# Weights of the top four experts computed behind the first one-hot, and the bias products of the down projection in four row groups

## The chip, the cores and the metric

One core of one Trainium2 chip. A time is the device time of one execution of the whole program in microseconds (us). All data are float32. One execution was also taken by the hardware profiler; the line numbers here are those of that profile.

## What is computed

One step of a decoder layer for 256 prompt tokens and 8 sample tokens, 264 rows in all: a token mixer (retention and gated delta net, with their input projection, branches and output projection), then a mixture of experts, of which the change touches the routing and the bias of the down projection:

```python
logits = x2 @ w_router + b_router                 # 264 x 32
top_v, top_i = lax.top_k(logits, 4)
gate = softmax(top_v)                             # weights of the 4 experts of a token
...
hb  = xb @ w_gate_up[e] + b_gate_up[e]            # 1024 -> 2048
glu = minimum(hb[:, :1024], 7.0)
lin = clip(hb[:, 1024:], -7.0, 7.0)
act = glu * sigmoid(1.702 * glu) * (lin + 1.0)
y   = act @ w_down[e] + b_down[e]                 # 1024 -> 1024
out[token] += gate[token, e] * y
```

The sum over a token's experts of gate * b_down[e] is Z @ b_down, where Z (264 x 32) holds the weights of the chosen experts and zeros elsewhere.

## The kernel before, in words

The program is written engine by engine, each with its own instruction stream in a hand-made order; semaphores order them. The first third is the token mixer. Out of it come `XT`, the residual with features in the partitions, in eight `out_block`s (L1042), and with each block a piece of the router's scores and of the sum of squares (`score`, L1051 and L1053), for which ACT squares `XT` (L1473). The tokens lie in three tiles c = 0, 1, 2 of 128, 128 and 8 rows.

**Routing.** ACT copies scores and sums out (`lgc`, L1475), PE turns them to tokens (L1085), ACT takes the roots of the mean squares into `rs` (L1479), DVE their reciprocals; ACT writes the normed rows `hrow` (L1488) and copies the residual to `X` (L1495). On DVE: `Lg` (L2073), the maxima, `ex` = logits less maximum (L2080), and the mask `sel` of the top four (L2091). From `sel`, PE counts each token's place in its expert's list (L1096, L1097) and the counts (L1100). ACT makes `ex` into exponentials (L1499). DVE makes Z from them (L2094 to L2097: mask, sum, reciprocal, product), then the places `R0` (L2101), the one-hot matrix `O` of block 0 (L2106) and the shifted tables `R` (15 instructions, L2113).

**Blocks.** Block b is 64 slots of expert b. `gather` (L1114) picks its rows with a one-hot; `turn_x` (L1122) transposes them; `gate_up` (L1136) multiplies by 8 chunks `gus` of 1 MB; DVE and ACT form the activation; `turn_act` (L1145), `down` (L1155) with 4 chunks `dns` of 1 MB; `turn_c` (L1165) and `combine` (L1180) spread the 64 rows, weighted, over the tokens in the banks `homes`, and DVE adds them to `X` (L2188). PE's order in iteration b is gate_up(b), turn_act(b-1), turn_c(b-2), gather(b+1), combine(b-2), turn_x(b+1), down(b-1). In iteration 1 nothing is there to combine, and `biases` (L1195) stands in its place: it multiplies ZT, the transposed Z, by `bd`, which holds b_down. ZT is made ahead of `gather(1)`: three transposes (L1208) into bank 6, and a copy by ACT (L1536).

**Loads.** All weights go through SP's queue in this order: `gus` and `dns` of blocks 0 and 1 as the token mixer frees their place, `bd` (L540) ahead of the last of them, then for each block `gus` (L519), the bias `bgu` (L523) and `dns` (L530). There is one set of eight `gus`: the chunk of block b + 1 is issued when gate_up(b) is through with the chunk in its place (`m_guc`). Of `dns` there are two sets; `down(b)` frees those of block b + 2 (`m_dc`). SP waits in order, so a wait for `m_dc` also holds all `gus` behind it.

ACT's functions need tables, and the program holds an ACT_TABLE_LOAD where the next function is not in the one loaded.

Of the kernel before, what the change touches and what calls it, by code (L numbers as in the profile page):

```python
# [14 lines left out]
ALU = mybir.AluOpType  # L15
ACT = mybir.ActivationFunctionType
# [3 lines left out]
AX = mybir.AxisListType  # L20

P = 128
D = 1024
KT = D // P
# [67 lines left out]
def build_layer(nc, d, o):  # L92

    with ExitStack() as ctx:
        base = [-(-nc.sbuf_base // 32) * 32]

        def at(name, offset, shape, dt=F32):
            return nc.alloc_sbuf_tensor_at(name, shape, dt, offset=offset)
# [114 lines left out]
        def mnew(name, shape, dt=F32):  # L213
            n = 4
            for x in shape[1:]:
                n *= x
            t = at(name, mb[0], shape, dt)
            mb[0] += -(-n // 32) * 32
            assert mb[0] <= p0 + PREG, mb[0]
            return t  # L220
# [27 lines left out]
        X, Xd = at("X", ht0, [P, 2, D]), at("Xd", wn0, [NB, D])  # L248
        bd = mnew("bd", [NE, D])
        bgu, ZT = at("bgu", xr0 + 4096, [1, 2, 2, 512]), at("ZT", ed0, [NE, TOK])  # L250
        sg, ac, acT, yb = [at(n, k0 + 4 * C_LVL + 2048 * i, [P, 512]) for i, n in enumerate(("sg", "ac", "acT", "yb"))]
# [128 lines left out]
        def after(eng, s, per, b, plus=0):  # L380

            if isinstance(b, int) and b * per + plus <= 0:
                return
            eng.wait_ge(s, b * per + plus)
# [24 lines left out]
        def _(sp):  # L410
# [128 lines left out]
            sp.wait_ge(s_mix, 8)  # L539
            sp.dma_start(bd[:, :], d["b_down"][0]).then_inc(s_bdn, 16)  # L540
            sp.wait_ge(s_bt, 20)
# [30 lines left out]
        def _(pe):  # L572
# [611 lines left out]
            def biases():  # L1184

                pe.wait_ge(s_ztev, 1)
                pe.wait_ge(s_bdn, 16)
                for c, r in TILES:
                    if c == 1:
                        pe.wait_ge(m_taev, 1)  # L1190
                        pe.wait_ge(m_gxev, 3)
                    elif c == 2:
                        pe.wait_ge(m_b2, 2)
                    for g in range(2):
                        t = pe.matmul(homes[c][g][0:r, :], ZT[:, P * c:P * c + r], bd[:, 512 * g:512 * g + 512],  # L1195
                                      start=True, stop=True)
                    t.then_inc(m_cb, 1)

            pe.wait_ge(s_xaev, 1)
# [7 lines left out]
            for c, r in TILES:  # L1207
                t = pe.transpose(B[6][0:NE, P * c:P * c + r], Z[0:r, c, :], K[0:r, C_ID:C_ID + r])  # L1208
            t.then_inc(s_zt, 1)
# [41 lines left out]
        def _(act):  # L1251
# [218 lines left out]
            for m in range(KT):  # L1470
                act.wait_ge(s_ob, m + 1)
                after(act, s_lg, 1, m - 1)
                nc.scalar.activation(sqt[:, m % 2, :], XT[:, m, :], ACT.Square).then_inc(s_sqt, 1)  # L1473
            act.wait_ge(s_lg, KT)
# [60 lines left out]
            act.wait_ge(s_zt, 1)  # L1535
            nc.scalar.copy(ZT[:, :], B[6][0:NE, 0:TOK]).then_inc(s_ztev, 1)  # L1536
            rows_out(1)
# [136 lines left out]
        def _(dve):  # L1674
# [417 lines left out]
            dve.wait_ge(s_sel, 1)  # L2092
            dve.wait_ge(s_ex, 1)
            link(v.tensor_tensor(ex[:, :, :], ex[:, :, :], sel[:, :, :], ALU.mult))  # L2094
            link(v.tensor_reduce(red[:, :], ex[:, :, :], AX.X, ALU.add))
            link(v.reciprocal(red[:, :], red[:, :]))
            v.tensor_tensor(Z[:, :, :], ex[:, :, :], bc(red[:, :], NE, 2), ALU.mult).then_inc(s_zg, 1)  # L2097

            dve.wait_ge(s_pos, 1)
# [11 lines left out]
            for c, r in TILES:  # L2111
                for m in range(NM):
                    t = v.tensor_scalar(R[0:r, c, NE * m:NE * m + NE], R0[0:r, c, :], -1000.0 - SLOTS * m, None,  # L2113
                                        ALU.add)
            t.then_inc(s_tab, 1)
            dve.wait_ge(s_tab, 3)

# [131 lines left out]
```

## Time and profile before

| | us |
|---|---|
| median of three runs | 1520.24 (1518.2 to 1521.64) |
| the profiled execution | 1520.41 |
| its span, which all views count from | 1518.5 |
| PE busy | 1426.2 |
| DVE busy | 509.3 |
| ACT busy | 247.0 |
| POOL busy | 141.6 |

PE is TensorE, PEld its weight loads, DVE VectorE, ACT ScalarE, POOL GpSimd, SP the engine whose queue issues the loads. A float32 matmul is two instructions (x2) in the views of the trace, a transpose is one.
### The profile page before, as it was taken

The numbers are of one execution on the slowest core, as the hardware profiler recorded it, in microseconds if no ns is written. First come the engines' busy times: TensorE is split into PE (matmuls) and PEld (weight loads), VectorE is DVE, ScalarE is ACT, GpSimd is POOL, SyncE is SP. The second block draws the span as 40 slices with busy tenths as digits, with TensorE's granted clock in tenths as the row PEclk, the third lists the DMA queues.
The fourth block names the chain that finished last, engine by engine and source line by source line (L and its number), as shares of the span: only waits on it lengthen the run. The fifth ranks groups of instructions, "written<-read, shape, count | busy, mean of one in ns | idle before, by whom it ended". The sixth has DMA issues, their size and how long they took to land.

```text
span 1518.5 us, 17635 instructions
## 1 busy us (share of the span) xinstructions
PE 1426.2 (94%) x7230; PEld 690.4 (45%) x7230; DVE 509.3 (34%) x1127; ACT 247.0 (16%) x456; POOL 141.6 (9%) x120
## 2 busy tenths in 40 slices
PE   7998998999999989999999999999999999999996
PEld 6787996448788623333333233233332332233222
DVE  5677534131402212832322242224222422242225
ACT  3342252002210310110110111011101110111012
POOL 1134011010000011001000100010001000100010
PEclk9999999999999998999999999999999999999998
DMA  6513045933546968999999999999999999999991
GB/s 203 211 58 105 35 141 167 292 140 125 181 153 255 357 246 336 417 418 415 417 417 418 415 417 419 417 415 417 418 417 415 416 418 418 415 417 418 417 412 68
DMA packets 129927, 480.46 MB, mean 316 GB/s; under 512 B 16841, under 2 KB 37593, under 8 KB 96777
## 3 DMA queue, kind: packets, MB, share of 16 engines
q1 hardware_dynamic: 129268, 478.68, 79.8%
q8 instruction: 59, 0.97, 0.3%
q0 software_dynamic: 96, 0.33, 0.1%
q10 hardware_dynamic: 480, 0.29, 0.1%
q14 instruction: 24, 0.20, 0.0%
HBM read 468.20 MB, written 11.26 MB: 316 GB/s over the span
## 4 chain that ended last, share of the span: by engine, by line
PE 44%; DMA 41%; SPq 5%; issue 5%; DVE 3%; ACT 1%; POOL 0%; DVEq 0%; ACTq 0%; POOLq 0%
DMA gus<-in_w_gate_up 39%; PE bank L1136 11%; PE bank L647 5%; PE bank L1155 4%; SPq L519 4%; PE bank L1019 4%; PE bank L889 3%; PE bank L620 3%; PE bank L1042 2%; PE bank L635 2%; PE bank L1114 2%; PE bank L1180 2%; DMA Ssg<-in_state_gdn 1%; DVE Ssg L1942 1%; SPq L457 1%
## 5 line engine op out<-in xcount | busy, mean ns | idle before, releaser
L1136 PE MATMUL bank<-gus,xT 128*64 128x512 f32 x2048 | 462.3, 598 | 39.6 <-DMA gus<-in_w_gate_up 37.2
L1136 PEld LDWEIGHTS bank<-gus,xT 128*64 128x64 f32 x2048 | 140.5, 137 | 355.5 <-issue 242.0
L2165 DVE TENSOR_TENSOR glu<-bank,bgb 128x512 f32<-128x512 f32 x32 | 22.1, 691 | 654.5 <-issue 419.1
L1155 PE MATMUL bank<-dns,acT 128*64 128x512 f32 x1024 | 229.2, 600 | 0.0
L1662 POOL PARTITION_BROADCAST bgb<-bgu x32 | 41.6, 1298 | 1042.1 <-DMA bgu<-in_b_gate_up 841.9
L1155 PEld LDWEIGHTS bank<-dns,acT 128*64 128x64 f32 x1024 | 71.2, 138 | 136.8 <-issue 136.8
L647 PE MATMUL bank<-HT,wslot 128*128 128x264 f32 x512 | 119.3, 388 | 0.0
L647 PEld LDWEIGHTS bank<-HT,wslot 128*128 128x128 f32 x512 | 95.3, 190 | 19.6 <-issue 4.6
L1114 PE MATMUL bank<-hrow,O 128*64 128x512 f32 (+1 forms) x384 | 95.4, 615 | 3.5 <-DVE O L2106 3.5
L1520 ACT COPY acT<-bank 128x512 f32<-128x512 f32 x32 | 18.8, 586 | 480.9 <-PE bank L1145 480.9
L1180 PE MATMUL bank<-yb,CT 64*128 64x512 f32 (+1 forms) x384 | 94.5, 607 | 1.7 <-ACT CT L1525 1.6
L635 PE MATMUL bank<-HT,wslot 128*128 128x264 f32 x384 | 89.5, 394 | 0.8 <-DVE HT L1709 0.8
L2188 DVE TENSOR_TENSOR X<-X,bank 128x512 f32<-128x512 f32 x132 | 81.7, 676 | 17.0 <-PE bank L1180 13.1
L635 PEld LDWEIGHTS bank<-HT,wslot 128*128 128x128 f32 x384 | 74.0, 194 | 15.3 <-issue 2.3
L889 PE MATMUL bank<-wslot,HT 128*128 128x512 f32 x128 | 58.9, 620 | 3.7 <-DMA wslot<-in_w_in 3.1
L1180 PEld LDWEIGHTS bank<-yb,CT 64*128 64x128 f32 (+1 forms) x384 | 25.2, 151 | 65.2 <-issue 63.3
L1530 ACT COPY yb<-bank 128x512 f32<-128x512 f32 x32 | 18.8, 587 | 214.1 <-PE bank L1155 214.1
L1114 PEld LDWEIGHTS bank<-hrow,O 128*64 128x64 f32 (+1 forms) x384 | 22.1, 135 | 49.5 <-issue 48.9
L1720 DVE SCALAR_TENSOR_TENSOR uT<-raw,cw,uT 128x256 f32<-128x256 f32 x72 | 42.8, 594 | 2.6
L2188 DVE TENSOR_TENSOR Xd<-Xd,bank 8x512 f32<-8x512 f32 x66 | 41.8, 669 | 2.2 <-PE bank L1195 2.2
L1666 POOL PARTITION_BROADCAST bgb<-bgu x32 | 41.6, 1300 | 6.4 <-POOL bgb L1662 6.4
L889 PEld LDWEIGHTS bank<-wslot,HT 128*128 128x128 f32 x128 | 25.1, 199 | 35.4 <-issue 30.7
(390 smaller groups left out, 1193.4 us busy)
## 6 DMA issues: line engine op xcount, KB each, us to landing
gus<-in_w_gate_up SPq DMA_DIRECT2D x256, 1024.0 KB, 20.6
dns<-in_w_down SPq DMA_DIRECT2D x128, 1024.0 KB, 22.2
wslot<-in_w_in SPq DMA_DIRECT2D x17, 2048.0 KB, 7.9
out<-Ssg SPq DMA_DIRECT2D x8, 512.0 KB, 6.1
Ssr<-in_state_ret SPq DMA_DIRECT2D x4, 1024.0 KB, 11.0
out<-Ssr SPq DMA_DIRECT2D x4, 1024.0 KB, 8.8
wslot<-in_w_branch_b SPq DMA_DIRECT2D x2, 2048.0 KB, 8.4
wslot<-in_w_branch_a SPq DMA_DIRECT2D x2, 2048.0 KB, 8.3
```

The costliest lines, as they stand in the source:

```text
L519: sp.dma_start(gus[k][:, :], expert(d["w_gate_up"], e)[P * k:P * k + P, :]).then_inc(m_wgu[k], 16)
L620: return lambda out, h: pe.matmul(out, lhsT(h), rhs(h), start=True, stop=True)
L635: ins = pe.matmul(B[t % 2][:, 0:TOK], wslot[u][:, k, P * m:P * m + P], HT[:, k, :], start=(k == 0), stop=(k == KT - 1))
L647: t = pe.matmul(B[n % 2][:, 0:TOK], wslot[u][:, k, P * m:P * m + P], HT[:, k, :], start=(k == 0), stop=(k == KT - 1))
L889: t = pe.matmul(banks[c][:, :], lhsT[:, k, P * c:P * c + P], w[:, k, :], start=(k == 0), stop=(k == KT - 1))
L1019: t = pe.matmul(B[m % 2][:, 0:TOK], wslot[r % 2][:, k, P * (m % 4):P * (m % 4) + P], (zT if m < KT else gT)[:, k, :], start=(k == 0), stop ...
L1114: t = pe.matmul(B[3][64 * g:64 * g + 64, :], O[0:r, c, :], hrow[0:r, c, 512 * g:512 * g + 512], start=(c == 0), stop=(c == 2))
L1136: t = pe.matmul(B[part][64 * g:64 * g + 64, :], block_of(xT, k), gus[k][:, D * part + 512 * g:D * part + 512 * g + 512], start=(k == 0), s ...
L1155: t = pe.matmul(B[2][64 * g:64 * g + 64, :], block_of(acT, k), dns[4 * u + k // 2][:, k % 2, 512 * g:512 * g + 512], start=(k == 0), stop= ...
L1180: t = pe.matmul(homes[c][g][0:r, :], CT[64 * g:64 * g + 64, P * c:P * c + r], yb[64 * g:64 * g + 64, :], start=True, stop=True)
L1720: v.scalar_tensor_tensor(acc, raw[:, t % 2, j:j + 256], cw[:, blk, j:j + 1], acc, ALU.mult, ALU.add).then_inc(s_cvc if j < 3 else s_cv, 1)
L2188: t = v.tensor_tensor(f, f, homes[c][g][0:r, :], ALU.add)
```

## The change

1. DVE no longer forms Z ahead of `R0`, `O` and `R`, but behind them.
2. ACT takes a root of the constant `eps` into a column of `red`, which is overwritten later, between two squares; the table of the root is loaded there.
3. `bd` is now 128 partitions by 512: partition group j of 32 holds the half j mod 2 of the columns of b_down, so both halves lie there twice. Four DMAs fill it.
4. ZT lies in 128 partitions, four copies of 32; Z is multiplied by the identity four times for each tile, once into each partition group of bank 6.
5. The bias products of tiles 0 and 1 read four different partition groups of ZT and `bd`, and all wait for `m_taev` and `m_gxev` first; those of tile 2 use groups 0 and 1.

```diff
--- before.py
+++ after.py
@@ -246,8 +246,8 @@
         WN = at("WN", xr0, [P, D])
         wr, br = at("wr", wn0, [P, KT, NE]), at("br", wn0 + 1024, [P, NE])
         X, Xd = at("X", ht0, [P, 2, D]), at("Xd", wn0, [NB, D])
-        bd = mnew("bd", [NE, D])
-        bgu, ZT = at("bgu", xr0 + 4096, [1, 2, 2, 512]), at("ZT", ed0, [NE, TOK])
+        bd = mnew("bd", [P, 512])
+        bgu, ZT = at("bgu", xr0 + 4096, [1, 2, 2, 512]), at("ZT", ed0, [P, TOK])
         sg, ac, acT, yb = [at(n, k0 + 4 * C_LVL + 2048 * i, [P, 512]) for i, n in enumerate(("sg", "ac", "acT", "yb"))]
         gus = [at(f"gus{k}", wreg + 8192 * k, [P, 2 * D]) for k in range(KT)]
         dns = [at(f"dns{k}", (wreg + 65536 if k < 4 else p0 - 32768) + 8192 * k, [P, 2, D]) for k in range(KT)]
@@ -537,7 +537,8 @@
             load_gate_up(0, 0, range(4, 8))
             load_down(1, 1, 1, None)
             sp.wait_ge(s_mix, 8)
-            sp.dma_start(bd[:, :], d["b_down"][0]).then_inc(s_bdn, 16)
+            for j in range(4):
+                sp.dma_start(bd[NE * j:NE * j + NE, :], d["b_down"][0][:, 512 * (j % 2):512 * (j % 2) + 512]).then_inc(s_bdn, 16)
             sp.wait_ge(s_bt, 20)
             load_gate_up(0, 0, range(2))
             sp.wait_ge(s_bt, 24)
@@ -1184,17 +1185,19 @@
             def biases():
 
                 pe.wait_ge(s_ztev, 1)
-                pe.wait_ge(s_bdn, 16)
-                for c, r in TILES:
-                    if c == 1:
-                        pe.wait_ge(m_taev, 1)
-                        pe.wait_ge(m_gxev, 3)
-                    elif c == 2:
-                        pe.wait_ge(m_b2, 2)
+                pe.wait_ge(s_bdn, 64)
+                pe.wait_ge(m_taev, 1)
+                pe.wait_ge(m_gxev, 3)
+                for c in range(2):
                     for g in range(2):
-                        t = pe.matmul(homes[c][g][0:r, :], ZT[:, P * c:P * c + r], bd[:, 512 * g:512 * g + 512],
-                                      start=True, stop=True)
+                        rows = slice(NE * (2 * c + g), NE * (2 * c + g) + NE)
+                        t = pe.matmul(homes[c][g][:, :], ZT[rows, P * c:P * c + P], bd[rows, :], start=True, stop=True)
                     t.then_inc(m_cb, 1)
+                pe.wait_ge(m_b2, 2)
+                for g in range(2):
+                    rows = slice(NE * g, NE * g + NE)
+                    t = pe.matmul(homes[2][g][0:NB, :], ZT[rows, 2 * P:TOK], bd[rows, :], start=True, stop=True)
+                t.then_inc(m_cb, 1)
 
             pe.wait_ge(s_xaev, 1)
             gather(0)
@@ -1205,7 +1208,9 @@
             pe.wait_ge(s_xaev, 4)
             pe.wait_ge(s_zg, 1)
             for c, r in TILES:
-                t = pe.transpose(B[6][0:NE, P * c:P * c + r], Z[0:r, c, :], K[0:r, C_ID:C_ID + r])
+                for j in range(4):
+                    t = pe.matmul(B[6][NE * j:NE * j + NE, P * c:P * c + r], Z[0:r, c, :], K[0:r, C_ID:C_ID + r],
+                                  start=True, stop=True)
             t.then_inc(s_zt, 1)
             gather(1)
             pe.wait_ge(s_xaev, 6)
@@ -1470,6 +1475,8 @@
             for m in range(KT):
                 act.wait_ge(s_ob, m + 1)
                 after(act, s_lg, 1, m - 1)
+                if m == KT - 1:
+                    nc.scalar.activation(red[:, 0:1], eps[:, :], ACT.Sqrt)
                 nc.scalar.activation(sqt[:, m % 2, :], XT[:, m, :], ACT.Square).then_inc(s_sqt, 1)
             act.wait_ge(s_lg, KT)
             nc.scalar.copy(lgc[:, :], B[2][0:64, 0:TOK]).then_inc(s_lgc, 1)
@@ -1533,7 +1540,7 @@
             x_out(0)
             residual_out(4, 6)
             act.wait_ge(s_zt, 1)
-            nc.scalar.copy(ZT[:, :], B[6][0:NE, 0:TOK]).then_inc(s_ztev, 1)
+            nc.scalar.copy(ZT[:, :], B[6][:, 0:TOK]).then_inc(s_ztev, 1)
             rows_out(1)
             sigmoid(0)
             x_out(1)
@@ -2090,12 +2097,6 @@
             link(v.tensor_tensor(eq[:, :, :], eq[:, :, :], R0[:, :, :], ALU.mult))
             v.tensor_tensor(sel[:, :, :], gt[:, :, :], eq[:, :, :], ALU.add).then_inc(s_sel, 1)
             dve.wait_ge(s_sel, 1)
-            dve.wait_ge(s_ex, 1)
-            link(v.tensor_tensor(ex[:, :, :], ex[:, :, :], sel[:, :, :], ALU.mult))
-            link(v.tensor_reduce(red[:, :], ex[:, :, :], AX.X, ALU.add))
-            link(v.reciprocal(red[:, :], red[:, :]))
-            v.tensor_tensor(Z[:, :, :], ex[:, :, :], bc(red[:, :], NE, 2), ALU.mult).then_inc(s_zg, 1)
-
             dve.wait_ge(s_pos, 1)
             for c, r in TILES:
                 t = v.scalar_tensor_tensor(R0[0:r, c, :], B[2][0:r, NE * c:NE * c + NE], 999.0, sel[0:r, c, :],
@@ -2113,6 +2114,11 @@
                     t = v.tensor_scalar(R[0:r, c, NE * m:NE * m + NE], R0[0:r, c, :], -1000.0 - SLOTS * m, None,
                                         ALU.add)
             t.then_inc(s_tab, 1)
+            dve.wait_ge(s_ex, 1)
+            link(v.tensor_tensor(ex[:, :, :], ex[:, :, :], sel[:, :, :], ALU.mult))
+            link(v.tensor_reduce(red[:, :], ex[:, :, :], AX.X, ALU.add))
+            link(v.reciprocal(red[:, :], red[:, :]))
+            v.tensor_tensor(Z[:, :, :], ex[:, :, :], bc(red[:, :], NE, 2), ALU.mult).then_inc(s_zg, 1)
             dve.wait_ge(s_tab, 3)
 
             def extras():
```

Where instructions moved, in the order of each engine. On DVE behind the mask, before (L2094 to L2097 form Z, L2101 `R0`, which the program lists as `R_156`, L2106 `O`, L2113 `R`):

```order
L2091 TENSOR_TENSOR sel<-gt,eq 128x96 [waits dve_chain]
L2094 TENSOR_TENSOR ex<-ex,sel 128x96 [waits s_ex,s_sel]
L2095 TENSOR_REDUCE red<-ex 128x3 [waits dve_chain]
L2096 RECIPROCAL red<-red 128x3 [waits dve_chain]
L2097 TENSOR_TENSOR Z<-ex,red 128x96 [waits dve_chain]
L2101 SCALAR_TENSOR_TENSOR R_156<-bank,sel 128x32 [waits s_pos]
L2101 SCALAR_TENSOR_TENSOR R_156<-bank,sel 128x32
L2101 SCALAR_TENSOR_TENSOR R_156<-bank,sel 8x32
L2106 TENSOR_SCALAR O<-K,R_156 128x64 [waits s_tab]
L2106 TENSOR_SCALAR O<-K,R_156 128x64
L2106 TENSOR_SCALAR O<-K,R_156 8x64
L2110 COPY cnt<-bank 1x32 [waits s_pos]
L2113 TENSOR_SCALAR R<-R_156 128x32 x10
L2113 TENSOR_SCALAR R<-R_156 8x32 x5
```

And now:

```order
L2098 TENSOR_TENSOR sel<-gt,eq 128x96 [waits dve_chain]
L2102 SCALAR_TENSOR_TENSOR R_156<-bank,sel 128x32 [waits s_pos,s_sel]
L2102 SCALAR_TENSOR_TENSOR R_156<-bank,sel 128x32
L2102 SCALAR_TENSOR_TENSOR R_156<-bank,sel 8x32
L2107 TENSOR_SCALAR O<-K,R_156 128x64 [waits s_tab]
L2107 TENSOR_SCALAR O<-K,R_156 128x64
L2107 TENSOR_SCALAR O<-K,R_156 8x64
L2111 COPY cnt<-bank 1x32 [waits s_pos]
L2114 TENSOR_SCALAR R<-R_156 128x32 x10
L2114 TENSOR_SCALAR R<-R_156 8x32 x5
L2118 TENSOR_TENSOR ex<-ex,sel 128x96 [waits s_ex]
L2119 TENSOR_REDUCE red<-ex 128x3 [waits dve_chain]
L2120 RECIPROCAL red<-red 128x3 [waits dve_chain]
L2121 TENSOR_TENSOR Z<-ex,red 128x96 [waits dve_chain]
```

The four instructions of Z, the first of which waits for the exponentials (`s_ex`), went behind `R`; `R0` now waits for PE's positions and the mask alone.

On ACT from the squares on, before:

```order
L1473 ACTIVATE sqt<-XT 128x264 [waits s_ob] x2
L1473 ACTIVATE sqt<-XT 128x264 [waits s_lg,s_ob] x6
L1475 COPY lgc<-bank 64x264 [waits s_lg]
L1479 ACT_TABLE_LOAD
L1479 ACTIVATE rs<-bank,eps 128x2 [waits s_lt]
L1479 ACTIVATE rs<-bank,eps 8x1
```

And now:

```order
L1480 ACTIVATE sqt<-XT 128x264 [waits s_ob] x2
L1480 ACTIVATE sqt<-XT 128x264 [waits s_lg,s_ob] x5
L1479 ACT_TABLE_LOAD [waits s_lg]
L1479 ACTIVATE red<-eps 128x1 [waits s_ob]
L1480 ACTIVATE sqt<-XT 128x264
L1482 COPY lgc<-bank 64x264 [waits s_lg]
L1486 ACTIVATE rs<-bank,eps 128x2 [waits s_lt]
L1486 ACTIVATE rs<-bank,eps 8x1
```

The table load left the place ahead of the roots of L1479 (now L1486) and stands ahead of a root of one column; it waits for `s_lg`, the root for `s_ob`, and the eighth square follows them.

On PE the bias products, before:

```order
L1195 MATMUL bank<-bd,ZT 128x512 [waits s_bdn,s_ztev]
L1195 MATMUL bank<-bd,ZT 128x512
L1195 MATMUL bank<-bd,ZT 128x512 [waits m_gxev,m_taev]
L1195 MATMUL bank<-bd,ZT 128x512
L1195 MATMUL bank<-bd,ZT 8x512 [waits m_b2]
L1195 MATMUL bank<-bd,ZT 8x512
```

And now:

```order
L1194 MATMUL bank<-bd,ZT 128x512 [waits m_taev,m_gxev,s_bdn,s_ztev]
L1194 MATMUL bank<-bd,ZT 128x512 x3
L1199 MATMUL bank<-bd,ZT 8x512 [waits m_b2]
L1199 MATMUL bank<-bd,ZT 8x512
```

The first row waits for all that tiles 0 and 1 need; after it four products of 128 rows follow one another without a wait.

## Rows read from the trace of the kernel before

**Rows 1.** The page, GB/s moved by DMA in 40 equal slices.

```profile
GB/s 203 211 58 105 35 141 167 292 140 125 181 153 255 357 246 336 417 418 415 417 417 418 415 417 419 417 415 417 418 417 415 416 418 418 415 417 418 417 412 68
```

**Rows 2.** Chain that ended last, at the roots and near the end: start us, us, what.

```profile
522.90 0.77 issue
...
1449.92 26.86 DMA gus<-in_w_gate_up
```

**Rows 3.** Stretches of 4 us: busy of PE, PEld, DVE, ACT, POOL; PEclk, DMA share, GB/s.

```profile
524.00:528.00 4.00, 3.13 (x23) 2.03 (x21) 3.45 (x18) 3.69 (x8) 0.00 (x0) 1.00 0.80 328
...
532.00:536.00 4.00, 2.41 (x6) 0.85 (x8) 2.72 (x25) 0.00 (x0) 0.00 (x0) 0.61 0.00 0
...
544.00:548.00 4.00, 4.00 (x20) 1.29 (x18) 0.00 (x0) 1.26 (x1) 0.00 (x0) 1.00 0.34 123
...
580.00:584.00 4.00, 4.00 (x7) 1.37 (x5) 1.28 (x2) 0.00 (x0) 0.00 (x0) 0.58 1.02 418
584.00:588.00 4.00, 4.00 (x5) 0.36 (x4) 1.28 (x2) 0.00 (x0) 0.00 (x0) 0.50 0.81 338
...
592.00:596.00 4.00, 4.00 (x16) 1.19 (x14) 0.00 (x0) 0.00 (x0) 0.00 (x0) 0.71 0.47 134
```

**Rows 4.** SP's queue in order of time: start us, us, line, operation.

```profile
503.36 17.69 SPq L519 DMA_DIRECT2D gus<-in_w_gate_up  x4
...
545.23 12.34 SPq L519 DMA_DIRECT2D gus<-in_w_gate_up  x8
...
593.02 6.24 SPq L530 DMA_DIRECT2D dns<-in_w_down  x4
```

**Rows 5.** ACT in order of time, same columns, idle before and its releaser in brackets.

```profile
522.37 1.28 ACT L1479 ACT_TABLE_LOAD   x1
523.67 0.40 ACT L1479 ACTIVATE rs<-bank,eps 128x2 f32<-128x2 f32 x2
...
579.23 0.59 ACT L1505 COPY xg<-bank 128x512 f32<-128x512 f32 x1 [1.17 <-PE bank L1114]
```

**Rows 6.** DVE in order of time, around the exponentials.

```profile
527.71 0.26 DVE L2091 TENSOR_TENSOR sel<-gt,eq 128x96 f32<-128x96 f32 x1
531.51 0.26 DVE L2094 TENSOR_TENSOR ex<-ex,sel 128x96 f32<-128x96 f32 x1 [3.54 <-ACT ex L1499]
...
532.47 0.37 DVE L2101 SCALAR_TENSOR_TENSOR R<-bank,sel 128x32 f32<-128x32 f32 x3
...
533.47 1.35 DVE L2113 TENSOR_SCALAR R<-R 128x32 f32<-128x32 f32 x15
```

**Rows 7.** PE in order of time, from the positions to down(0).

```profile
529.02 0.22 PE L1097 MATMUL bank<-sel,K 8*8 8x32 f32 x2
...
533.59 4.25 PE L1114 MATMUL bank<-hrow,O 128*64 128x512 f32 x12 [3.46 <-DVE O L2106]
...
539.96 0.49 PE L1208 MATMUL bank<-K,Z 128*32 128x128 f32 x3
540.38 2.94 PE L1114 MATMUL bank<-hrow,O 128*64 128x512 f32 x12
...
579.11 9.22 PE L1195 MATMUL bank<-bd,ZT 32*128 32x512 f32 x12
...
589.30 9.55 PE L1155 MATMUL bank<-dns,acT 128*64 128x512 f32 x32
```

**Rows 8.** PE: prices of column and row groups, timeline, then the chain.

```profile
22.42 1.10 PE L600 MATMUL bank<-HT,wab 128*32 128x264 f32 x16
...
400.22 1.15 PE L983 MATMUL bank<-dq,kms 32*128 32x256 f32 x16
401.30 3.83 PE L647 MATMUL bank<-HT,wslot 128*128 128x264 f32 x16
...
207.68 1.78 PE bank L620 x16
...
619.88 7.02 PE bank L1155 x32
```

## Prediction

> **What bounds the kernel now.** I read the page's 40 slices first. From slice 16 of 40 (607 us) to the last but one, the DMA engines move 412 to 419 GB/s whatever the other engines do; before that the numbers are uneven [rows 1]. The chain that ended last agrees: in its last half it is a row of loads of `gus`, 25 to 27 us long each, one for a block, with little between them [rows 2]. So the end is the start of a full-rate stream plus its bytes. A faster matmul behind 607 us buys nothing; what buys time is DMA idle time that goes away before that.
>
> The table by stretch shows that idle time [rows 3]. The stream slows in 524 to 528 and stands still until 544 to 548 (123 GB/s in 4 us, at 418 GB/s that is 1.2 us of work, so it resumes at 546.8). It runs full from there, and stops again at 587.2 (338 GB/s in 584 to 588 is 3.2 us of work), to resume at 594.7 (134 GB/s in 592 to 596 is 1.3 us). I call them gap 1 and gap 2; gap 2 is 7.5 us. Between them lie 40.4 us of full-rate traffic, the 16 MB of gate/up weights of blocks 1 and 2.
>
> What ends each gap is in the queue of SP [rows 4]. Gap 1 ends when the first product of block 0, at L1136, frees `gus`: the first reload is issued at 545.23, data flow 1.6 us later. Gap 2 ends when the first quarter of `down(0)`, L1155, frees `dns`: issued at 593.02, flowing 1.7 us later. What the change touches lies in front of these two points.
>
> **The change, part by part.**
>
> *The square root's table.* Before, ACT loads it at 522.37 behind the copy of `lgc`, and the root starts at 523.67 [rows 5]. The scores' transposes were through at 522.90 and the chain counts 0.77 us of mere issue from there [rows 2]: that is what the load costs. In the changed order the load waits for the product of score 5, and falls between two squares while PE still has out block 7 to do (3.8 us), so it is covered. The new root of one column waits for `s_ob` and stands ahead of the last square. The two roots after the load took 0.40 us together, so I give the new one 0.2 us, of which 0.1 us is covered because PE is at the row transposes. Gain: 0.65 us. Without that cover it would be 0.55.
>
> *First one-hot ahead of the weights.* `sel` is written at 527.71, and DVE then stands for 3.54 us until ACT has the exponentials; the four instructions of Z, then L2101, and `gather(0)` on PE follow at 533.59 [rows 6, 7]. What L2101 itself needs is the last L1097, which ended at 529.24. It could start at 529.30 in place of 532.47: 3.17 us. PE's own counts (L1100) had ended 3.46 us before `gather(0)`, at 530.1 [rows 7], or 529.5 with the 0.65, and `gather(0)` would come at 529.8: they don't hold it up. Z now stands behind the 15 instructions of R (1.35 us [rows 6]). With both shifts, R ends near 531.1, the exponentials are there at 530.8, and Z, a microsecond of work, is ready at 532.1. PE asks for it behind `gather(0)` and two sets of transposes, at about 535. Three microseconds of cover hide it; the second one-hot, which is queued behind Z on DVE, waits for `gather(0)` anyway.
>
> *The clock at `gather(0)`.* That group took 4.25 us, the same group for block 1 2.94 us [rows 7]. In front of the first PE was idle for 3.46 us, and the granted clock of 532 to 536 is 0.61 [rows 3], so a good part of the group ran at 1.2 GHz. With 0.3 us of idle time left I expect 2.4 GHz: 1.31 us more. The bounds are 0 and 1.31.
>
> *Z transposed into four partition groups.* Three transposes took 0.42 us [rows 7]. Now they are 12 matmuls, eight of 128 columns. The only matmuls into four column groups in the trace are those of L600: eight of 264 columns, 2112 in all, in 1.10 us [rows 8]. 1024 columns are then 0.5 us, the four 8-column ones at most 0.2. That is 0.7, or 0.3 more than now; I take 0.4. If they ran one by one, L620's rate of eight 128-column matmuls in 1.78 us [rows 8] gives 2.0 us, 1.6 more. The nearest row is L600, with the same groups.
> The Trainium skill (TensorE: Matmul & The Clock Gate, Terms) says of the transpose mode that it is "4× faster for FP32", which speaks against giving it up. Here a transpose of 128 columns took a third of 0.42 us and L620 0.22 us, 1.5 times as much, so the trace does not bear it out; by the rule the eight would be 1.2 us in two sets of four, and the time 0.5 us longer.
>
> So `gate_up(0)` comes earlier by 0.65 + 3.17 + 1.31 - 0.4 = **4.7 us**, and so does the end of gap 1, one for one: the weights of block 0 had all landed by 528 [rows 3] and are needed from 538.5.
>
> *The load of `bd`.* Four issues in place of one, 256 KB in place of 128 KB: 0.3 us at 418 GB/s. They stand ahead of the first gate/up loads, but those are issued over 17.7 us and waited for `s_bt` [rows 4], and the queue had emptied 11 us before the first use. Nothing. Without that cover it costs 0.3 us and three issues.
>
> *The bias products.* From L1195 at 579.11 to L1155 at 589.30 are 10.2 us, and 13.9 us to the first freed `dns` [rows 7, 4]. Six matmuls of 32 rows run one after the other, and the granted clock fades under them: 0.58 in 580 to 584, then 0.50 until down is well under way [rows 3]. Now four matmuls stand in four row groups and write to four banks. The row to price them by is L983, eight matmuls of 32 rows by 256 columns in four row groups into four banks: from 400.22 to L647 at 401.30 [rows 8], 1.08 us for 2048 columns. L647 needs 3.76 us for 2112 one by one. The bias products of c = 0 and 1 are 4 x 512 = 2048 columns: 1.1 us. The two for c = 2 go in a pair, as the six of L1114 do in 2.94: 1.0 us.
> Their wait moves ahead: it now holds c = 0 too until ACT has copied `xg` of block 2, from 579.23 for 0.59 us [rows 5]. That is 0.7 us of idle PE. Only this and the transposes of turn_x(2) are queued behind it.
> At 2.4 GHz the way from the start of the biases to the first freed `dns` is 0.7 + 1.1 + 1.0 + 0.6 (four transposes, half of what they took at 1.2 GHz) + a quarter of 7.02 (down at 2.4 GHz [rows 8]) = 5.2 us, in place of 13.9. It starts at 579.1 - 4.7 = 574.4, so the load is issued at 579.6 and flows at 581.3. The traffic already queued lasts until 587.2 - 4.7 = 582.5. **Gap 2 closes whole**, with 1.2 us to spare, and gives its 7.5 us. PE gains more (some 14 us up to `gate_up(2)`), which it only spends in waiting sooner for weights.
>
> *Sum:* 4.7 + 7.5 = 12.2 us, out of 1520.41 us for the profiled execution (span 1518.5 and 1.9 around it): 1508.2. The median shown is 0.2 lower; forecast **1508.0 us**.
>
> **The rivals.**
> - *The clock still falls at the biases.* For it: it fell within 2 us of their start, and it fell after the 2.3 us pause ahead of `gate_up(1)` too; the new pause of 0.7 us and the half-filled pair remain. Against: they last 2 us in place of 9, two times as dense and more. Then the way is 0.7 + 2 x 4.5 = 9.7 us, data flow at 585.8, and 3.3 us of gap 2 stay: 12.2 - 3.3, **1511.3 us**. Chance 0.18.
> - *The row groups don't overlap, so that the change doesn't do what it says.* L983 speaks against it. Then the old 13.9 us and the 0.7 us of wait: gap 2 grows by 0.7, gain 4.7 - 0.7 = 4.0, **1516.2 us**. Chance 0.06.
> - *Routing gains little, because gather(0) or its clock is held by something that I don't see*; only gap 2 closes: **1512.7 us**. Chance 0.06.
> - *Slower: the clock falls and stays at 1.2 GHz through down(0) and gate_up(2).* Down(0) then takes 14.0 us, gate_up(2) 27.5 us, from 594.4 to 621.9; the next `dns` is freed only 9 us of products later, near 630.9, flowing at 632.5. Before, 12 MB after 594.7 reached 624.8, so the stream is 7.7 us behind: **1527.9 us**. It decides from a low clock of about 27 us on. The rows show recovery within 5 us of dense work, both at `gather(0)` and at down(0) (0.71 in 592 to 596). Chance 0.03.
>
> **How the numbers follow.** The forecast has the rest, 0.67, of which I keep 0.04 for gains that vanish in something not seen. A measurement can tell 0.2%, 3 us, from no change. Faster by more: 0.63 + 0.18 + 0.06 + 0.06 = 0.93, less 0.01 for the serial case coming out smaller: 0.92. Within: 0.05. Slower: 0.03. The range: the lower end is the sum without the charge for Z and with 1.5 us for the scatter of three runs (1518.2 to 1521.64), 1506; the upper takes in the clock's rival and L620's price for Z, 1511.3 + 1.2, and the routing rival: 1513. Outside are the serial case, no change and slower, 0.13 to 0.15.
>
> **What would show it.** ACT: a table load between the squares of L1480, none at L1486. DVE: L2102 some 0.1 us behind the last L1098, no wait of 3.5 us. PE: `gather(0)` near 529.8, some 2.9 us long; `gate_up(0)` near 538.5; L1194 and L1199 together about 2 us from 575.1, clock 1.00; down(0) 7.0 us. DMA: resuming near 542, then no 4 us stretch under 380 GB/s up to the end, whose rate is again 415 to 418 GB/s. It would be wrong if the stream's rate fell, if gap 2 stayed at full length, or if L1194 took over 4 us.

## The result, and the profile after

The changed kernel takes **1510.18 us** (median of four runs, 1508.32 to 1513.36) against 1520.24 us: the ratio is 0.9935, with a 95% interval of 0.9919 to 0.9951. That is 10.1 us faster, where 12.2 us was forecast (1508.0 us), and inside the range of 1506 to 1513. The profiled execution is the slowest of the four, 1513.36 us with a span of 1511.4 us, so it explains 7.1 us. The other 3 us are found further down, in later profiles of the same kernel.

The page's row of GB/s, in slices of 37.8 us now. From slice 16 on it reads as in [rows 1]; the two slices ahead of it rose.

```profile
GB/s 197 220 58 95 46 130 167 288 158 126 168 167 226 392 250 385 418 416 414 418 418 416 416 418 417 416 416 417 417 417 416 417 417 417 415 418 417 417 410 66
```

The stretches of 4 us (busy of PE, PEld, DVE, ACT, POOL; PEclk, DMA share, GB/s), against [rows 3]:

```profile
524.00:528.00 4.00, 3.52 (x31) 2.84 (x28) 3.45 (x18) 3.69 (x8) 0.00 (x0) 1.00 1.01 422
528.00:532.00 4.00, 3.63 (x24) 2.52 (x26) 2.57 (x24) 3.38 (x6) 0.00 (x0) 0.88 0.07 27
532.00:536.00 4.00, 3.22 (x10) 0.47 (x7) 1.16 (x6) 0.58 (x1) 0.00 (x0) 0.69 0.00 0
...
540.00:544.00 4.00, 4.00 (x20) 1.19 (x22) 0.00 (x0) 1.87 (x2) 0.00 (x0) 1.00 0.13 16
544.00:548.00 4.00, 4.00 (x22) 1.40 (x20) 0.00 (x0) 0.00 (x0) 2.32 (x2) 1.00 0.86 350
...
576.00:580.00 4.00, 3.22 (x16) 0.44 (x12) 2.59 (x8) 0.58 (x1) 0.00 (x0) 0.85 1.02 422
580.00:584.00 4.00, 4.00 (x12) 1.49 (x12) 3.20 (x8) 0.58 (x1) 0.00 (x0) 0.50 1.01 414
584.00:588.00 4.00, 4.00 (x18) 1.32 (x16) 0.00 (x0) 0.00 (x0) 1.77 (x2) 0.79 0.52 165
588.00:592.00 4.00, 4.00 (x22) 1.26 (x18) 0.00 (x0) 0.58 (x1) 0.83 (x1) 1.00 1.01 412
592.00:596.00 4.00, 4.00 (x20) 1.26 (x18) 0.00 (x0) 0.00 (x0) 0.00 (x0) 1.00 0.94 336
```

Gap 1 now ends in 544 to 548, where 350 GB/s are 3.35 us of work at 418: the stream resumes at 544.7, 2.1 us earlier than before. Gap 2 has shrunk: 165 GB/s in 584 to 588 leave 2.4 us idle, in place of 7.5. A new small hole follows in 592 to 596, 336 GB/s, 0.8 us: the four `dns` are through before `gate_up(2)`, which starts at 590.4, has freed its first chunk. Two stretches have a low clock where I expected 1.00: 532 to 536, at `gather(0)`, and 580 to 584, at the biases.

DVE around the mask, against [rows 6]:

```profile
527.72 0.26 DVE L2098 TENSOR_TENSOR sel<-gt,eq 128x96 f32<-128x96 f32 x1
529.36 0.37 DVE L2102 SCALAR_TENSOR_TENSOR R<-bank,sel 128x32 f32<-128x32 f32 x3 [1.39 <-PE bank L1098]
529.77 0.57 DVE L2107 TENSOR_SCALAR O<-K,R 128x64 f32<-128x64 f32 x3
...
530.36 1.35 DVE L2114 TENSOR_SCALAR R<-R 128x32 f32<-128x32 f32 x15
531.63 0.24 DVE L2118 TENSOR_TENSOR ex<-ex,sel 128x96 f32<-128x96 f32 x1
...
532.41 0.26 DVE L2121 TENSOR_TENSOR Z<-ex,red 128x96 f32<-128x96 f32 x1
```

L2102 starts 0.1 us behind the positions, Z (L2118 to L2121) is written at 532.7. ACT around the roots, against [rows 5]:

```profile
517.18 0.42 ACT L1480 ACTIVATE sqt<-XT 128x264 f32<-128x264 f32 x1 [3.90 <-DVE XT L2071]
517.63 1.28 ACT L1479 ACT_TABLE_LOAD   x1
521.51 0.20 ACT L1479 ACTIVATE red<-eps 128x1 f32<-128x1 f32 x1 [2.60 <-DVE XT L2071]
521.62 0.41 ACT L1480 ACTIVATE sqt<-XT 128x264 f32<-128x264 f32 x1
522.78 0.37 ACT L1482 COPY lgc<-bank 64x264 f32<-64x264 f32 x1 [0.76 <-PE bank L1054]
523.68 0.40 ACT L1486 ACTIVATE rs<-bank,eps 128x2 f32<-128x2 f32 x2 [0.53 <-PE bank L1086]
```

The table load (L1479) falls between two squares, while PE has out block 7 to do. The new root takes 0.20 us, and the square starts at 521.62.

PE, against [rows 7], and SP's two issues that end the gaps, against [rows 4]:

```profile
530.48 4.59 PE L1115 MATMUL bank<-hrow,O 128*64 128x512 f32 x12 [0.34 <-DVE O L2107]
...
537.28 0.82 PE L1212 MATMUL bank<-K,Z 128*32 128x128 f32 x24
538.03 2.94 PE L1115 MATMUL bank<-hrow,O 128*64 128x512 f32 x12
540.90 13.95 PE L1137 MATMUL bank<-gus,xT 128*64 128x512 f32 x64
...
577.60 1.14 PE L1194 MATMUL bank<-bd,ZT 32*128 32x512 f32 x8 [0.78 <-ACT xg L1512]
578.67 1.77 PE L1199 MATMUL bank<-bd,ZT 32*8 32x512 f32 x4
580.38 1.12 PE L1123 MATMUL bank<-K,xg 128*128 128x128 f32 x4
581.42 9.17 PE L1156 MATMUL bank<-dns,acT 128*64 128x512 f32 x32
```

```profile
542.88 12.35 SPq L519 DMA_DIRECT2D gus<-in_w_gate_up  x8
...
585.15 5.86 SPq L530 DMA_DIRECT2D dns<-in_w_down  x4
```

Both ends of the gaps moved with the issue: 545.23 to 542.88, and 593.02 to 585.15.

Executions differ in the token mixer ahead of all this by up to 4 us, a part that the change does not touch. So I count from the end of the last score product (the last L1053 or L1054), which lies at 521.94 before and 522.74 here. In the table, all times are us from there, worked out from each kernel's PE rows; "end" is the span less that point. "Old" biases are the six products in one row group, "new" the six in four groups.

| kernel (profile) | gather(0) starts, takes | gate_up(0) starts | biases, us | down(0) starts, takes | end |
|---|---|---|---|---|---|
| before | 11.65, 4.25 | 21.31 | old, 9.22 | 67.36, 9.55 | 996.6 |
| changed | 7.74, 4.59 | 18.16 | new, 1.14 and 1.77 | 58.68, 9.17 | 988.7 |
| changed, second | 7.74, 4.93 | 20.89 | new, 1.14 and 1.03 | 58.51, 7.09 | 988.9 |
| changed, third | 7.74, 4.59 | 18.16 | new, 1.14 and 1.03 | 57.47, 7.09 | 986.1 |
| e1, order and table | 7.74, 4.59 | 17.74 | old, 8.60 | 63.17, 8.47 | 992.1 |
| e2, bias part | 11.64, 4.42 | 21.88 | new, 1.14 and 1.03 | 61.10, 7.09 | 991.3 |
| e3, table | 10.86, 4.93 | 21.20 | old, 8.44 | 66.46, 8.63 | 995.3 |
| e4, late biases | 7.74, 4.59 | 18.16 | none here | 55.36, 7.09 | 986.1 |
| e5, filler | 8.12, 2.94 | 18.17 | new, 1.14 and 1.03 | 57.48, 7.09 | 985.9 |
| e6, spare PE work | 7.75, 4.99 | 20.90 | new, 1.14 and 1.03 | 58.52, 7.09 | 990.3 |
| e7, late and filler | 8.13, 2.94 | 18.18 | none here | 55.38, 7.09 | 986.3 |
| e8, filler, Z early | 8.12, 2.94 | 16.99 | new, 1.14 and 1.03 | 54.61, 7.09 | 985.2 |
| e9, e8 and late | 8.12, 2.94 | 16.99 | none here | 52.49, 7.09 | 985.0 |

### The profile page after: what moved, and what is told of

Same layout as the page of the kernel before. It is cut to its first block, busy times and chain, and to the rows that moved or that the text cites. A ratio compares the mean times of both kernels' runs of the same rounds, so it can differ in the third digit from the quotient of the medians.

```text
span 1511.4 us, 17681 instructions
## 1 busy us (share of the span) xinstructions
PE 1419.1 (94%) x7251; PEld 688.0 (46%) x7251; DVE 508.8 (34%) x1127; ACT 247.0 (16%) x457; POOL 141.5 (9%) x120
## 4 chain that ended last, share of the span: by engine, by line
PE 44%; DMA 42%; SPq 5%; issue 5%; DVE 3%; ACT 1%; POOL 0%; DVEq 0%; ACTq 0%; POOLq 0%
DMA gus<-in_w_gate_up 39%; PE bank L1137 11%; PE bank L648 5%; PE bank L1156 4%; SPq L519 4%; PE bank L1020 4%; PE bank L890 3%; PE bank L621 3%; PE bank L1043 2%; PE bank L636 2%; PE bank L1115 2%; PE bank L1181 2%; DMA Ssg<-in_state_gdn 1%; DVE Ssg L1949 1%; DMA wslot<-in_w_in 1%
## 6 DMA issues: line engine op xcount, KB each, us to landing
Ssr<-in_state_ret SPq DMA_DIRECT2D x4, 1024.0 KB, 11.4
```

## The experiments

**Each part alone.** e1 has the order and the table, with the biases of before:

```diff
+                if m == KT - 1:
+                    nc.scalar.activation(red[:, 0:1], eps[:, :], ACT.Sqrt)
...
-            dve.wait_ge(s_ex, 1)
-            link(v.tensor_tensor(ex[:, :, :], ex[:, :, :], sel[:, :, :], ALU.mult))
...
             dve.wait_ge(s_pos, 1)
...
             t.then_inc(s_tab, 1)
+            dve.wait_ge(s_ex, 1)
+            link(v.tensor_tensor(ex[:, :, :], ex[:, :, :], sel[:, :, :], ALU.mult))
...
```

> The routing part alone: Z behind the one-hot, and the root's table between the squares; the bias products and their loads are those of before. Theory (the time is DMA idle time ahead of a full-rate stream): gather(0) starts 3.9 us earlier relative to the last score product, and gate_up(0) and the end of gap 1 follow, by 3.5 to 5 us, less if the clock falls again at gather(0); gap 2 keeps its 7.5 us, because the biases and down(0) shift along with it. Ratio 0.997 to 0.998, 1515.5 to 1517. Rival (the whole gain of 10 us comes from the biases, and routing is hidden by something): ratio 1.000.

Measured: 1514.86 us against 1520.44, ratio 0.9966 (0.9954 to 0.9978), 5.6 us, just under the 1515.5 to 1517 expected; by their profiles the ends in the table are 4.5 us apart. PE in its profile:

```profile
527.93 4.59 PE L1114 MATMUL bank<-hrow,O 128*64 128x512 f32 x12 [0.34 <-DVE O L2102]
...
573.78 8.60 PE L1195 MATMUL bank<-bd,ZT 32*128 32x512 f32 x12
...
583.36 8.47 PE L1155 MATMUL bank<-dns,acT 128*64 128x512 f32 x32
```

`gather(0)` starts 7.74 us behind the last score product, in place of 11.65: the 3.9 us of the theory. It takes 4.59 us, so the clock fell again (0.54 in 528 to 530). The old biases take 8.6 us, and 6.7 us of gap 2 are left. The rival (routing is hidden) falls.

e2 is the changed kernel with these two edits (the order on DVE and the table) undone.

> The bias part alone: four row groups, Z transposed four times, four loads of b_down; the routing order and the root's table are those of before. Theory: gate_up(0) comes 0.4 us later (the 24 small matmuls of Z), the biases take 2 to 3 us in place of 9.2 behind a wait of 0.7 us, and gap 2 shrinks from 7.5 to between 0 and 3.5 us: ratio 0.9955 to 0.9975, 1513.5 to 1516.5. With e1 it sums to the whole change. Rival (the two parts need one another): the sum of the two gains falls short of 10 us by more than 2 us.

Measured: 1514.85 us, ratio 0.9960 (0.9946 to 0.9974), 5.6 us. In its profile the biases take 1.14 and 1.03 us, and down(0) runs in 7.09 us. gate_up(0) starts 21.88 us behind the last score, 0.57 later than before: Z's 24 small instructions, and a `gather(0)` that happened to be 0.2 us longer. The sum of the two gains, 11.2 us, is that of the whole change (10.1) within the intervals, so the parts don't need one another.

e3 has the table alone.

> Only the square root's table is loaded between the squares; everything else is the kernel before. Theory: the roots at L1479 start 0.7 to 0.8 us sooner behind the last score, but DVE's one-hot is still behind the exponentials, which are behind the copies on ACT's queue, so the shift is passed on whole: 0.7 us, ratio 0.9995, not to be told from none. Rival (the loads of tables cost more than their row shows, as an engine may have to drain at each): 2 us or more, ratio 0.9985 or less.

Measured: 1518.92 us, ratio 0.9991 (0.9982 to 1.0000). The profile gives the price: `gather(0)` starts 10.86 in place of 11.65 us behind the last score, 0.79 us. Its clock took 0.68 us of that back in this execution, and most of the 1.3 us by which its end is sooner comes from a shorter gap 2. The median moved by 1.5 us. The rival's 2 us or more are inside the interval, so the time alone does not exclude them, but the rows speak against them: before, the first root started at 523.67, right behind the load that ran from 522.37 for 1.28 us [rows 5].

**Where the biases stand.** e4 takes them out of iteration 1, and puts them and DVE's additions behind down(15), with semaphores of their own:

```diff
                 else:
-                    biases()
+                    pe.sem_inc(m_cb, 3)
...
                 down(b - 1, (b - 1) % 2, 16 * ((b - 1) // 2) + 16)
+                if b == LATE:
+                    biases(b)
```

> The whole change, with the bias products and their additions moved from iteration 1 to iteration 16, behind down(15), where PE waits for weights anyway. Nothing is left out. Theory: gap 2 closes, since down(0) starts some 3 us sooner and its first dns is freed ahead of the time when the queue is empty; in iteration 16 PE and DVE have 2 us of products and 4 us of additions more, which the lead of the loads covers. 2 to 4 us faster than the changed kernel: ratio 0.991 to 0.992, 1506.5 to 1508. Rival (what is left of gap 2 in the changed kernel costs nothing, since the stream makes it up): the same as the changed kernel, 0.9935. Rival (the pause in iteration 16 starves the stream): slower than the changed kernel.

Measured: 1510.98 us, ratio 0.9939 (0.9925 to 0.9952): no faster than the changed kernel. The profile does what the theory says. In iteration 1 and then in iteration 16:

```profile
576.04 0.66 PE L1125 MATMUL bank<-K,xg 128*128 128x128 f32 x4 [0.69 <-ACT xg L1515]
576.63 7.09 PE L1158 MATMUL bank<-dns,acT 128*64 128x512 f32 x32
```

```profile
1025.76 1.03 PE L1194 MATMUL bank<-bd,ZT 32*8 32x512 f32 x4
1026.72 1.14 PE L1199 MATMUL bank<-bd,ZT 32*128 32x512 f32 x8
1030.55 9.64 PE L1139 MATMUL bank<-gus,xT 128*64 128x512 f32 x36 [2.70 <-DVE X L2220]
```

down(0) starts 3.3 us sooner than in the changed kernel's first profile, and no 2 us stretch between 544 and 640 is under 380 GB/s. In iteration 16 PE stands for 2.7 us behind DVE's additions, and the stream does not notice: no stretch of 4 us from 640 to 1460 falls below 380 GB/s. The 2 to 4 us that I expected did not come. The likely reason is that gap 2 was closed in most executions of the changed kernel already, and that only those like its first profile had something left to win. That asked for more profiles of the changed kernel.

> The changed kernel once more, on the chip of e5 to e7, since its first profile was the slowest of its four runs. Theory (the clock at the biases falls in some executions and not in others, as it did in the first profile and did not in e2's): a median of 1509.5 to 1511, and, if the profile catches an execution without the fall, gap 2 closed and a span 3 us shorter than the first profile's. Rival (the first profile is typical): 1512 to 1514.

Measured: 1510.37 us (1506.23 to 1512.01), ratio 0.9932 (0.9918 to 0.9946). Gap 2 is closed in its profile, but the low clock at `gather(0)` lasted longer (0.50 in 530 to 538, 0.53 in 538 to 540), so gate_up(0) came 2.7 us later than in the first profile, and the ends, 988.7 and 988.9, are nearly the same. The changed kernel a third time, beside e8 and e9:

> The changed kernel on the chip of e8 and e9, as their measure: 1509.5 to 1511, ratio 0.993 to 0.994.

Measured: 1510.57 us, ratio 0.9943 (0.9930 to 0.9957). PE in the third profile:

```profile
530.30 4.59 PE L1115 MATMUL bank<-hrow,O 128*64 128x512 f32 x12 [0.34 <-DVE O L2107]
...
537.10 0.82 PE L1212 MATMUL bank<-K,Z 128*32 128x128 f32 x24
...
577.41 1.14 PE L1194 MATMUL bank<-bd,ZT 32*128 32x512 f32 x8 [0.78 <-ACT xg L1512]
578.49 1.03 PE L1199 MATMUL bank<-bd,ZT 32*8 32x512 f32 x4
...
580.03 7.09 PE L1156 MATMUL bank<-dns,acT 128*64 128x512 f32 x32
```

Here the biases are through in 2.1 us and down(0) takes 7.09 us, at 2.4 GHz. In both later profiles no 2 us stretch between 552 and 640 is under 380 GB/s: gap 2 is closed whole, as forecast. The third one's end is 986.1, as e4's. Over all profiles with the new biases in iteration 1 the clock fell at them in one of seven, the first; with the old ones in three of three.

**What the end hangs on.** e6 gives PE idle products in the second half of the stream:

```diff
+                if b >= 16:
+                    spare(3)
```

`spare(3)` is three products of 128 rows by 256 columns into bank 7.

> The changed kernel with three idle products of 128 rows by 256 columns more in each of the iterations 16 to 31, 1.3 us each time, 20 us of PE work in all. Their results are not used. Theory (behind about 770 us the stream of weights sets the end, and PE's 2.4 us of waiting in each block covers the extra work): the changed kernel's time, up to 2 us more for what lies in the last block. Rival (PE is the bound and the stream follows it): 20 us slower.

Measured: 1511.35 us, ratio 0.9942 (0.9928 to 0.9957), 1.0 us above the changed kernel in the same comparison. The stretch from 1200 to 1450, in e6 and then in the changed kernel's second profile:

```profile
1200.00:1450.00 250.00, 244.21 (x1129) 85.00 (x1127) 71.44 (x154) 27.98 (x50) 20.75 (x16) 1.00 1.02 417
```

```profile
1200.00:1450.00 250.00, 236.81 (x1082) 75.54 (x1080) 71.63 (x156) 27.74 (x51) 20.75 (x16) 1.00 1.02 417
```

PE is busy 7.4 us more, and the stream is at 417 GB/s in both. A group of three takes 1.30 us up to the next instruction, 21 us for the 16 groups; the busy time of PE over the whole span rose by only 11.8 us (1418.0 to 1429.8), and why it rose by so much less stays open. By either count the added work cost about one microsecond, so PE is not the bound there: the rival falls. Most of the microsecond lies behind the stream, where one of the groups stands: from the last eight instructions of gate_up(31) to the end of the span are 42.5 us in e6, and 41.4 and 41.7 in the changed kernel's second and third profile.

**The clock at gather(0).** In e5 the counts go behind `gather(0)`, and wide products fill their place:

```diff
+            pe.wait_ge(s_hrev, 6)
+            pe.matmul(B[7][:, 0:256], ident, XT[:, 0, 0:256], start=True, stop=True)
             pe.wait_ge(s_sel, 1)
...
-            for c, r in TILES:
-                t = pe.matmul(B[1][:, 0:NE], K[0:r, C_ONE:C_ONE + P], sel[0:r, c, :],
...
+            pe.matmul(B[7][:, 0:512].rearrange("p (a n) -> p a n", a=2), ident, XT[:, 2:4, 0:256], start=True, stop=True)
...
             gather(0)
+            for c, r in TILES:
+                t = pe.matmul(B[1][:, 0:NE], K[0:r, C_ONE:C_ONE + P], sel[0:r, c, :],
...
```

> The changed kernel with PE kept at wide work around the positions: the counts of L1101, which gather(0) does not need, go behind it; in their place stands one product of 128 rows by 512 columns of the residual with the identity, and one of 256 columns ahead of the positions, both into bank 7, which is overwritten later. Nothing is left out. In the traces so far gather(0) took 4.3 to 4.9 us at 1.2 GHz even where PE had stood still for only 0.3 us. Theory (the clock falls because the work of the last microseconds is narrow or small, and not because of the pause alone): with the filler the clock stays at 2.4 GHz, gather(0) takes 2.9 us, gate_up(0) comes 1.5 us sooner, and the median is 1 to 2 us below the changed kernel's. Rival (only the pause or the place in time counts): gather(0) takes 4.6 us again and the time is the changed kernel's, within 0.5 us.

Measured: 1510.31 us, ratio 0.9937 (0.9924 to 0.9949), the changed kernel's time and not the 1 to 2 us less that I expected.

```profile
527.69 0.70 PE L1094 MATMUL bank<-XT,K 128*128 128x256 f32 x2 [0.45 <-ACT hrow L1499]
...
529.27 1.13 PE L1102 MATMUL bank<-XT,K 128*128 128x512 f32 x2
530.58 2.94 PE L1114 MATMUL bank<-hrow,O 128*64 128x512 f32 x12 [0.18 <-DVE O L2111]
...
537.01 0.82 PE L1216 MATMUL bank<-K,Z 128*32 128x128 f32 x24 [1.14 <-DVE Z L2125]
```

The clock stayed: `gather(0)` takes 2.94 us, at 2.4 GHz. The filler changes two things, though. It puts wide products among the narrow ones, and it shortens PE's two pauses, from 0.51 and 0.34 us to 0.45 and 0.18, so e5 alone does not show which of the two holds the clock. e2 bears on it, where the products of 32 columns (L1097 to L1101) run from 529.33 to 531.67 and the pause of 3.22 us follows them:

```profile
529.20:531.00 1.80, 1.67 (x16) 1.51 (x16) 0.08 (x1) 1.80 (x5) 0.00 (x0) 1.00 0.05 23
531.00:531.60 0.60, 0.60 (x4) 0.49 (x3) 0.00 (x0) 0.58 (x2) 0.00 (x0) 0.57 0.00 0
```

The clock is down (0.57) while the narrow products still run, ahead of the long pause, with only 0.51 us of idle time right in front of them. And the pause of 0.78 us ahead of the new biases, which stands behind the wide products of a gather, left the clock at 1.00 when they started, in all seven profiles. So the narrow work counts, and the long pause is not needed. No run has the narrow work without any pause.

But the gain went into a new wait: the counts come later, DVE copies them ahead of R and Z, and PE stands 1.14 us for Z at L1216. gate_up(0) starts at 18.17 us, where it did in the first and third profile.

e7 joins e4 and e5.

> The late bias products of e4 and the filler of e5 together. Nothing is left out. Theory: gap 2 stays closed whatever the clock does, and gap 1 ends 1.5 us sooner than in e4 if the filler holds the clock: 1 to 2 us under e4, ratio 0.9925. Rival: the same as e4, 0.994.

Measured: 1510.08 us, ratio 0.9932 (0.9920 to 0.9944). The rival holds (e4's ratio was 0.9939): e7 has e5's wait for Z, and its end is 986.3.

e8 mends that wait:

```diff
             t.then_inc(m_O, 1)
+            dve.wait_ge(s_ex, 1)
+            link(v.tensor_tensor(ex[:, :, :], ex[:, :, :], sel[:, :, :], ALU.mult))
...
             dve.wait_ge(s_pos, 2)
             v.tensor_copy(cnt[:, :], B[1][0:1, 0:NE]).then_inc(s_tab, 1)
...
-            dve.wait_ge(s_ex, 1)
-            link(v.tensor_tensor(ex[:, :, :], ex[:, :, :], sel[:, :, :], ALU.mult))
...
```

> e5 with DVE's four instructions of Z put back ahead of the copy of the counts and of R, but still behind the one-hot of block 0. Nothing is left out. In e5 the filler held the clock, but the counts came later, R and Z with them, and PE stood 1.14 us ahead of the transposes of Z, so gate_up(0) came 18.2 us after the last score product, as in the changed kernel where its clock fell for a short while (18.2 us; 20.9 us where it fell for long). Theory: Z no longer waits for the counts, the pause goes, and gate_up(0) comes 17.0 us after the last score product; the median is 1 us under e5 and 1 to 3 us under the changed kernel, 1507.5 to 1509.5, ratio 0.992 to 0.993. Rival (the first third of the program scatters more than that, and the gain cannot be told): within 0.5 us of the changed kernel.

Measured: 1509.17 us (1506.62 to 1510.10), ratio 0.9929 (0.9915 to 0.9942).

```profile
530.97 2.94 PE L1114 MATMUL bank<-hrow,O 128*64 128x512 f32 x12 [0.18 <-DVE O L2111]
...
536.20 0.82 PE L1216 MATMUL bank<-K,Z 128*32 128x128 f32 x24
536.97 2.94 PE L1114 MATMUL bank<-hrow,O 128*64 128x512 f32 x12
539.84 13.95 PE L1136 MATMUL bank<-gus,xT 128*64 128x512 f32 x64
```

The wait is gone, gate_up(0) starts 16.99 us behind the last score product, as expected. It is 1.4 us under the changed kernel beside it (1510.57), with intervals that overlap. e9 adds the late biases:

> e8 with the late bias products of e4. Nothing is left out. Theory: as e8, and gap 2 is closed in every execution and not only in those where the clock holds at the biases: 0 to 1.5 us under e8, ratio 0.992. Rival: the same as e8.

Measured: 1508.99 us (1506.77 to 1510.14), ratio 0.9934 (0.9920 to 0.9948): e8's time. Both medians are below all three of the changed kernel (1510.18, 1510.37, 1510.57). By the traces they start the stream 1.2 us sooner than its best profile, but these runs alone don't settle that they are faster.

## Why the prediction was nearly right

- *The bound* was right: DMA idle time ahead of a full-rate stream. The sum can be made from the table for each profile: what gate_up(0) gained plus what gap 2 lost. For the third profile of the changed kernel that is 3.15 + 7.5 = 10.65 us, and the end moved by 10.4; for the first 3.15 + 7.5 - 2.4 - 0.8 = 7.45, and it moved by 7.9; for e8 4.32 + 7.5 = 11.8 and 11.4. In e1 and e3 the slow stretch at the old biases was a little shorter, and 0.8 and 1.1 us of gap 2 went: 3.57 + 0.8 = 4.4 against 4.5, and 0.11 + 1.1 = 1.2 against 1.3. For the second profile it is 0.42 + 7.5 = 7.9, and 7.7. Only e2 misses, -0.57 + 7.5 = 6.9 against 5.2. Most of its 1.7 us were lost behind the full-rate stream: in stretches of 2 us the rate first falls under 380 GB/s 40 us ahead of the end of the span before, and 42 us ahead of it in e2. Why, stays open.
- *The table*: 0.65 us forecast, 0.79 measured in e3. The 0.1 us that I charged for the late square was not there.
- *The order*: 3.17 us forecast; together with the table `gather(0)` was to come 3.82 us sooner and came 3.91 sooner.
- *The clock at gather(0)* is the term that failed. "With 0.3 us of idle time left I expect 2.4 GHz: 1.31 us more." The idle time was 0.34 us, and the clock fell all the same: 4.59 us in place of 2.94, in other executions 4.93, and then the low clock lasted through the transposes and into `gather(1)` and took gate_up(0) to 20.9 us. I read the fall in [rows 7] as the work of the 3.46 us pause. What the profiles show is that the long pause is not needed: in six of six profiles in which 0.34 us were left and no filler stood there `gather(0)` took 4.59 to 4.99 us, no less than the 4.25 to 4.93 of the three with a pause of 3.2 to 3.5 us, and in four of four with the filler 2.94. By e2, the run of products with 32 columns behind a pause of 0.51 us is enough. My bound of 0 for this term was no bound either, since the term ran from -0.3 to -3.1 us when the transposes and gather(1) are counted.
- *Z in four groups*: 0.4 us forecast over the old transposes. From their start to `gather(1)` are 0.75 us in place of 0.42, 0.33 more; from `gather(0)` to gate_up(0) the third profile takes 0.42 us more than e1's. It was never waited for in the changed kernel: Z was written at 532.7, and PE asked at 537.3.
- *The loads of `bd`* cost nothing that can be seen.
- *The biases*: 1.1 + 1.0 us forecast from L983 and L1114; 1.08 (from L1194 to L1199 in the third profile) and 1.03 (L1199 itself). The four row groups overlap, so the second rival falls. The wait for `xg` in front was 0.78 us, 0.7 forecast.
- *Gap 2* closed whole in every profile but one of those with the new biases. In that one the first rival happened, the clock fell during the pair of tile 2, and it cost 3.2 us, for which I had 3.3. Its profile was the first, which made the mechanism look likelier than it is.
- *The slower rival*: the clock came back 7 us after it fell at the biases (0.50 in 580 to 584, 0.79 in 584 to 588), far from the 27 us that it needed.

The step of the prediction that failed is thus this one term, the clock at `gather(0)`: forecast +1.3 us, measured -0.3 in the better executions, which is 1.6 of the missing 2 us. With the 0 that I gave as its lower bound the sum would have come to 1509.3 us, 0.9 from the measured time. The rest of the mechanism held. How many executions behind a median have the short low clock and how many the long one is not shown, since only profiled executions tell it.

## What to carry to other kernels

Where the second half of a program is a stream at the memory's rate, list the stretches in which the stream stands still, find for each the one instruction whose end frees the next load, and count a change by how far it moves these instructions; e6 shows how to test it, by giving the other engine work that should cost nothing. A low clock behind a pause is not proof that the pause made it: look at how wide the work ahead of it was, and at when the clock fell, before a gain is booked for the pause going away. Where a filler needs room, look at what waits for the work that it pushes back: in e5 that ate the whole gain.

## What was not expected of the hardware

- The granted clock went from 2.4 to 1.2 GHz at 531.0 in the changed kernel, after two pauses of 0.51 and 0.34 us with products of 32 columns between them, and it did so in each of the six profiles of the new order without wide products there. With a product of 256 and one of 512 columns among them, and pauses of 0.45 and 0.18 us, it stayed in four of four.
- An engine that is busy throughout can lose the clock too: six products of 32 rows, one after the other, had PE busy for all of 580 to 588 at 0.58 and 0.50 [rows 3]. The same products in four row groups kept 2.4 GHz in six of seven profiles.
- Four products of 32 rows by 512 columns in four row groups took 1.07 us in the first profile. By an estimate from L647's rate, 2112 columns of 128 rows in 3.83 us [rows 8], they would take 3.7 us one by one: 3.5 times as long.
